# Two pairs of prompt blocks through the experts as a dense product over both tables, the other blocks by gathers

## The reference

```python
def peer_ffn(h, w_query, sub_keys, u_table, v_table):      # 1024 prompt tokens + 32 samples
    q = (hf @ w_query).reshape(-1, 8, 2, 128)
    s = einsum('nhpk,hpmk->nhpm', q, sub_keys)             # 8 heads, 2 halves, 128 keys
    sv, si = top_k(s, 16)
    comb = sv[:, :, 0, :, None] + sv[:, :, 1, None, :]     # 16 x 16 sums per head
    cidx = si[:, :, 0, :, None] * 128 + si[:, :, 1, None, :]
    fv, fpos = top_k(comb, 16)
    eid, gate = take(cidx, fpos), softmax(fv)
    # for each block of 128 tokens
    a = einsum('phkd,pd->phk', u_table[eid], h)            # u_table, v_table: 16384 x 1024
    act = gelu(a) * gate
    return einsum('phk,phkd->pd', act, v_table[eid])
```

## Time and profile before

| | |
|---|---|
| median of 3 runs | 3471.02 us (3469.92 to 3482.42) |
| span of the profiled execution | 3289.1 us |
| median less span | 181.9 us |
| busy: PE, DVE, POOL, ACT | 2159.5, 2139.4, 2280.5, 368.6 us |
| moved by DMA | 1235.08 MB, of which gathers 1109.40 MB |
| mean granted TensorE clock | 0.823 |

### The profile page before, as it was taken

One profiled execution on the slowest core, in us unless ns is written; L12 is line 12 of the kernel. 1 busy time (PEld: TensorE's weight loads), 2 busy tenths in 40 slices (PEclk: granted clock), 3 DMA queues, 4 the chain that ended last, 5 costly groups with the idle time before them and its releaser, 6 DMA issues.

```text
span 3289.1 us, 30699 instructions
## 1 busy us (share of the span) xinstructions
PE 2159.5 (66%) x9831; PEld 958.8 (29%) x9831; DVE 2139.4 (65%) x4892; ACT 368.6 (11%) x793; POOL 2280.5 (69%) x2229
## 2 busy tenths in 40 slices
PE   6885896756776468997855577767454445545556
PEld 5573442212443113453211143434111111111111
DVE  1577756676788855666575657877766666677431
ACT  2112231100010110222100100001000000000000
POOL 0144677776777777777776777777777777777765
PEclk9997998977887789999877688889767777667679
DMA  8778899999999999999999999999999999999998
GB/s 290 202 273 299 326 385 386 388 401 401 397 395 389 360 396 406 405 405 386 382 400 394 375 399 390 392 382 370 369 405 406 402 402 406 406 385 402 382 363 321
DMA packets 363454, 1235.08 MB, mean 376 GB/s; under 512 B 36855, under 2 KB 40335, under 8 KB 363279
## 3 DMA queue, kind: packets, MB, share of 16 engines
q0 software_dynamic: 304784, 1109.40, 87.4%
q1 hardware_dynamic: 36335, 79.69, 6.8%
q10 hardware_dynamic: 22176, 44.04, 3.6%
HBM read 1220.31 MB, written 13.28 MB: 375 GB/s over the span
## 4 chain that ended last, share of the span: by engine, by line
POOL 29%; DMA 27%; PE 24%; issue 11%; DVE 7%; DVEq 1%; ACT 1%; SPq 0%; POOLq 0%; ACTq 0%
DMA v_ring<-in_v_table_dram,eidt 21%; POOL u_ring L807 15%; POOL v_ring L827 14%; PE bank L1758 13%; DMA u_ring<-in_u_table_dram,eid 4%; PE bank L1586 3%; PE bank L1668 2%; DVE u_ring L1381 2%; PE bank L1569 2%; PE bank L1644 2%; DMA u_ring<-in_v_table_dram,eidt 1%; DVE mixt L1211 1%; DVE work L1272 0%; DMA u_ring<-in_w_ada_dram 0%; POOL u_ring L827 0%
## 5 line engine op out<-in xcount | busy, mean ns | idle before, releaser
L1758 PE MATMUL bank<-v_ring,act_x 128*32 128x512 f32 x4104 | 1177.7, 808 | 977.7 <-DMA v_ring<-in_v_table_dram,eidt 929.9
L1381 DVE CUSTOM_DVE_ANT_0 u_ring<-u_ring,h 128x1024 f32<-128x1024 f32 x1056 | 1279.5, 1226 | 785.4 <-DMA u_ring<-in_u_table_dram,eid 711.9
L807 POOL DMA_INDIRECT u_ring<-in_u_table_dram,eid x1024 | 1129.9, 1103 | 444.0 <-issue 312.2
L827 POOL DMA_INDIRECT v_ring<-in_v_table_dram,eidt x1026 | 1070.3, 1043 | 397.3 <-issue 245.8
L1758 PEld LDWEIGHTS bank<-v_ring,act_x 128*32 128x32 f32 x4104 | 271.4, 135 | 1794.3 <-issue 1785.0
L1668 PEld LDWEIGHTS bank<-hbuf,wring 128*128 128x128 f32 x1984 | 228.4, 194 | 22.0 <-issue 22.0
L1668 PE MATMUL bank<-hbuf,wring 128*128 128x128 f32 (+1 forms) x1984 | 234.4, 279 | 0.0
L1586 PE MATMUL bank<-zc,dring 128*128 128x384 f32 x496 | 193.3, 514 | 4.0 <-ACT dring L860 4.0
L1569 PE MATMUL bank<-hbuf,wring 128*128 128x384 f32 (+2 forms) x448 | 150.8, 495 | 22.7 <-DMA wring<-in_w_in_dram 13.7
L1644 PE MATMUL bank<-wring,mixt 128*128 128x512 f32 (+1 forms) x256 | 123.2, 631 | 0.0
L1569 PEld LDWEIGHTS bank<-hbuf,wring 128*128 128x128 f32 x448 | 85.7, 194 | 89.7 <-issue 50.8
(11 more groups left out here) (267 smaller groups left out, 1696.6 us busy)
## 6 DMA issues: line engine op xcount, KB each, us to landing
v_ring<-in_v_table_dram,eidt POOLq DMA_INDIRECT x1026, 6.9
u_ring<-in_u_table_dram,eid POOLq DMA_INDIRECT x1024, 6.8
wring<-in_w_out_dram ACTq DMA_DIRECT2D x16, 1024.0 KB, 11.9
wring<-in_w_query_dram ACTq DMA_DIRECT2D x16, 1024.0 KB, 11.7
wring<-in_w_in_dram ACTq DMA_DIRECT2D x10, 1024.0 KB, 11.8
xr<-in_x_prompt_dram SPq DMA_DIRECT2D x16, 512.0 KB, 7.4
v_ring<-in_w_ada_dram SPq DMA_DIRECT2D x7, 1024.0 KB, 13.4
wring<-in_w_ada_dram SPq DMA_DIRECT2D x5, 1024.0 KB, 5.6
```

Source lines behind the costliest of these rows:

```text
L807: pool.indirect_dma_start(u_ring[:, n % NU], None, u_table[0], bass.IndirectOffsetOnAxis(ap=col, axis=0)).then_inc(u_in[n % NU], 16)
L827: pool.indirect_dma_start(place, None, v_table[0], bass.IndirectOffsetOnAxis(ap=eidt[:, b % RING, t:t + 1], axis=0)).then_inc(landed, 16)
L1381: dve.tensor_tensor_reduce(u_ring[:, n % NU], u_ring[:, n % NU], h2[:, b % 2], 1.0, 0.0, ALU.mult, ALU.add, dot[:, b % 2, k:k + 1]).then_i ...
L1758: last = pe.matmul(acc[h][j * S:(j + 1) * S, :], act_x[:, i % 2, j, a:a + S], v_place(n)[0][:, h * HALF:(h + 1) * HALF], start=(c == 0), s ...
```

## The change

Blocks 2 and 3 are one **dense pair**, blocks 6 and 7 another. They are no longer gathered. Blocks 0, 1, 4, 5 and SB keep the path above (`POS`), so the loop has 160 slots. For a dense pair (256 tokens) there are two stages, put into slots by `lay_out_dense` behind the last step of mixer and queries:

- **Units** (64, ten to a slot). A unit makes the gates of 4 tokens as a 128x128 table of first and second key each. VectorE makes gate-weighted one-hot columns of the first key (4 instructions), ScalarE those of the second as relu(1 - |key - number|) (4 of 128x128 and one of 128x512), TensorE multiplies them (4 matmuls 128x128), ScalarE copies the bank into a stage of 16 tokens. Each full stage (1 MB) is stored to DRAM by SP in runs of 512 B; there are two stage buffers.
- **Rounds** (134, seven to a slot). A round loads 128 rows of u and of v (0.5 MB each), transposes the u tile in two halves (one bank, 7, each half copied out by ScalarE), multiplies it with the 256 tokens (8 matmuls of 256 columns into bank 6), applies gelu, multiplies on VectorE by the gates read back (1 MB per 8 rounds), and adds the product with the v tile into banks 2 to 5 (4 matmuls of 512 columns). The v product runs 6 rounds behind the load, the dots 3.

The token matmuls of a slot are split around half of its dense work. Mixer and queries are packed closer: `ROOM` is 12 and 13, most gaps are shorter, both halves of the key search stand in the slot of the scores. The v ring has 5 rows, the sixth keeps the dense pair's keys and gates. VectorE now runs the steps of the same slot as TensorE, where it was one slot behind (`DVE_LAG`). The end of each dense block (`finish`) stands in the same order of ends as those of the gathered blocks.

```diff
-NV = 6
+NV = 5
-ROOM = [None, 7, 4.6]
+ROOM = [None, 12, 13]
+POS = [0, 1, 4, 5, SB]
+DENSE = [[2, 3], [6, 7]]
+UNIT = 4
+STOK = 16
+GEN_UNITS, ROUNDS = (10, 10), (7, 7)
...
+def lay_out_dense(steps):
+    at = max(s for s, todo in enumerate(steps) if any(x[0] not in pieces for x in todo)) + 2
+    for r, bs in enumerate(DENSE):
+        at = max(at, max(s for s, todo in enumerate(steps) if ("nrm", PARTS - 1, bs[-1]) in todo) + 2)
+        slots[at] += [("numbers", r, q) for q in range(NDB)]
+        for u in range(NUNIT):
+            slots[at + u // GEN_UNITS[r]].append(("unit", r, u))
...
+        for m in range(NROUND):
+            slots[at + m // ROUNDS[r]].append(("round", r, m))
...
+            def unit(r, u):
+                pe.wait_ge(oh_i_ready, n + 1)
+                pe.wait_ge(oh_j_ready, n + 1)
+                if n >= 4:
+                    pe.wait_ge(unit_taken, n - 3)
+                for i in range(UNIT):
+                    last = pe.matmul(ps[2 + n % 4][:, i * P:(i + 1) * P], oh_j[:, n % 2, i], oh_i[:, n % 2, i], start=True, stop=True)
+            def tile_turned(n, h):
+                if n + h:
+                    pe.wait_ge(ut_ready, 2 * n + h)
+                for a in range(4):
+                    last = pe.transpose(ps[7][:, a * P:(a + 1) * P], ud[n % NUD][:, (4 * h + a) * P:(4 * h + a + 1) * P], ident[:, :])
+            def dense_round(r, m, s):
+                for h in range(2):
+                    if m < NTILE:
+                        tile_turned(r * NTILE + m, h)
+                    if 0 <= m - VD_LAG < NKEY:
+                        dense_values(r, m - VD_LAG, h)
+                if 0 <= m - NDB - 1 < NKEY:
+                    dense_dots(r, m - NDB - 1, s)
...
+            def second_keys(r, u):
+                for i in range(UNIT):
+                    act.activation(oh_j[:, n % 2, i], iota_e, ACT.Abs, bias=gij[:, q, 2, t + i:t + i + 1])
+                if u:
+                    unit_out(r, u - 1)
+                act.drain()
+                act.activation(oh_j[:, n % 2], oh_j[:, n % 2], ACT.Relu, bias=one_c, scale=-1.0).then_inc(oh_j_ready, 1)
...
+            def dense_weights(r, m):
+                    dve.wait_ge(ge_ready, n + 1)
+                    dve.tensor_tensor(w, w, gch[c % 2].rearrange("p b t i c -> p (b t) i c")[:, :, i % IC], ALU.mult).then_inc(wd_ready, 1)
```

More of the change, by code:

```diff
@@ L161, in lay_out @@
 def lay_out():
-    slots = [[] for _ in range((NB + 1) * NCH)]
+    slots = [[] for _ in range(NSLOT)]
     load = [0] * len(slots)
@@ L204, in spread @@
             last = int(at)
-            if i[0] == "turn" and (last - V_LAG) % LAG > LAG - 5:
+            if i[0] == "turn" and (last - V_LAG) % LAG > LAG - 6:
                 last = at = last + LAG - (last - V_LAG) % LAG
@@ L418, in build @@
+        ud_in = [sem(f"ud_in{i}") for i in range(NUD)]
+        vd_in = [sem(f"vd_in{i}") for i in range(NVD)]
+        ut_ps, ut_ready, a_ps, ge_ready, wd_ready, vd_ps, dacc_free = (
+            sem(n) for n in ("ut_ps", "ut_ready", "a_ps", "ge_ready", "wd_ready", "vd_ps", "dacc_free"))
         steps = lay_out()
-        DVE_LAG = 1
+        dense, dense_ends = lay_out_dense(steps)
+        ends, END_ORDER = lay_out_ends(dense_ends)
+        END_NO = {x: i for i, x in enumerate(END_ORDER)}
+        END_BLOCK = [POS[x[1]] if x[0] == "row" else DENSE[x[1]][x[2]] for x in END_ORDER]
@@ L421, in build, with dots_before, turns_before @@
         SPREAD_AT = (0, 1)
-        turned = [sum(1 for s_ in range(V_LAG + LAG * i) for step in steps[s_] if step[0] == "turn") for i in range(2 * NB)]
-        turned.append(2 * NB + 1)
+        def dots_before(s):
+            return sum(1 for todo in dense[:s] for x in todo if x[0] == "round" and 0 <= x[2] - NDB - 1 < NKEY)
+        def turns_before(s):
+            return sum(1 for todo in steps[:s] for x in todo if x[0] == "turn")
+        turned = [sum(1 for s_ in range(V_LAG + LAG * i) for step in steps[s_] if step[0] == "turn") for i in range(2 * NPP)]
@@ L1454, in _ @@
             norm(1)
-            for p in range(NB + 1):
+            for p in range(NPP + 1):
                 for c in range(NCH):
-                    if p < NB or c < NSG:
-                        chunk(p, c)
-                    slot = p * NCH + c - DVE_LAG
-                    for step in steps[slot] if slot >= 0 else []:
+                    todo = dense[p * NCH + c]
+                    for end in ends[p * NCH + c]:
+                        finish(end)
+                    for j in range(CH):
+                        if p < NPP or c < NSG:
+                            dots(p, c, j, j + 1)
+                        for step in todo[j * len(todo) // CH:(j + 1) * len(todo) // CH]:
+                            dense_step(*step)
+                    dve.drain()
+                    for step in steps[p * NCH + c]:
                         kind = step[0]
@@ new lines, in dense_dots @@
+            def dense_dots(r, i, s):
+                n = r * NKEY + i
+                pe.wait_ge(act_taken, halves(s))
+                pe.wait_ge(eidt_ready, turns_before(s))
+                pe.wait_ge(ut_ready, 2 * (r * NTILE + NDB + i + 1))
+                if n:
+                    pe.wait_ge(ge_ready, n)
+                for k in range(KC):
+                    last = pe.matmul(ps[6][:, DT:2 * DT], ut[i % 2][:, k * P:(k + 1) * P], ht[:, k, :], start=(k == 0), stop=(k == KC - 1))
+                last.then_inc(a_ps, 1)
@@ L1815, in _ @@
             modulation(11)
-            for p in range(NB + 1):
+            for p in range(NPP + 1):
                 for c in range(NCH):
+                    todo = dense[p * NCH + c]
+                    if p == NPP and c == NSG + 2:
+                        weights(NPP, 0, p * NCH + c)
                     if v_chunk(p * NCH + c):
```

519 lines of the change are left out of this document (409 added, 110 removed).

## The result

The changed kernel takes 4607.16 us, median of 4 runs (4603.28 to 4609.07), where before took 3470.47 (3461.77 to 3482.42): a ratio of 1.3269 [1.3224, 1.3313]. The prediction was 4512 us, 4300 to 4800. The profiled execution took 4608.27 us with a span of 4606.1.

The account below looks back on a forecast made before the run. It took the gather stream to bound the kernel before and TensorE the rounds after. 195.5 head + 1420 slots + 205 units + 1148 rounds + 205 units + 1105 rounds + 52 end = 4330 us, plus 182 gives 4512; range 4300 to 4800.

Parts of the forecast that it names:

- Rounds, 8.0 us each: Dense rounds: TensorE needs 3.50 us of dots, 3.56 of value matmuls and 0.95 of transposes, 8.0 us a full round.
- starts and ends: Round stages: 35 and 25 us for starts and waits, plus 10 and 4 us as the ends' share.
- handshake rival: Rounds: with one bank each for transposes and dots, 1.6 us a round of ScalarE stand bare; 4920 us, chance 0.09.
- clock rival: Rounds: each half tile's wait drops TensorE to 1.2 GHz half the time, 1000 us more; 5500 us, chance 0.03.
- The other side: Rounds: 128-column matmuls go two at a time, a round takes 4.5 us; 3610 us, at best 3420; chance 0.03.
- Slots 0 to 97, 1420 us: Slots before the dense stages: each slot goes at its longest engine, adding to 1509 us; taken as 1420, 1230 to 1560.
- the rings: Slots 0 to 97: rings of 5 and 6 rows let an engine run about a slot ahead, smoothing some of 1509 us.
- rival of better smoothing: Slots 0 to 97 go at VectorE's own sum, 1230 us; the kernel takes 4320 us, chance 0.15.
- Units, 205 us a stage: Unit stages: ScalarE longest at 2.7 us a unit; 12.8 us taken per 1 MB gate buffer filled, 205 us a stage.
- rival of slow stores: Units: stores in 512 B runs take 22 us per 1 MB stage buffer and bind; 4810 us, chance 0.08.
- Around the span, 182 us: Outside the span: 3471.0 less 3289.1 us, 181.9 us, kept as a fixed cost and added to the forecast span.
- turning point: Rounds: the round time, about 4.2 us, from which the prediction said it decides whether the change could be faster than before.

Follow-up runs that it names:

- e2: Changed kernel with the dots of a round over 4 of the 8 pieces of the contraction: 4140.01 us against 4587.
- e12: Changed kernel with the dots of a round as bfloat16 matmuls on bfloat16 copies of u tiles and tokens: 3930.64 us against 4587.
- e3: Changed kernel loading only 64 of 1024 columns of the table tiles beyond the first of each buffer: 4590.24 us against 4587.
- e6: Changed kernel with VectorE running the steps of the slot before, as before the change: 4490.63 us against 4587.
- e7: Changed kernel with POOL issuing a slot's v gathers ahead of its u gathers: 4510.93 us against 4587.
- e9: Changed kernel with three edits, later copy in the units, VectorE a slot behind and v gathered first: 4460.25 us against 4587.
- e5: The changed kernel, unchanged, run again beside the kernel before on the chip of the later runs: 4586.91 us, ratio 1.3897.
- e4: Changed kernel with ScalarE copying out the bank of the unit before the last, not of the last: 4482.46 us against 4587.
- e8: Changed kernel with the copy of a unit's bank written straight, so gates are stored in another order: 4525.61 us against 4587.
- e1: The kernel before, unchanged, with span and time from one execution: 3299.38 us with a span of 3297.4.

## Why the prediction was right, and where it was not

**The bound.** Right: the change takes 200 MB off a stream which was the bound and puts some 2000 us of float32 matmuls (256 x 6.88 + 260 x 0.88) on TensorE, which has no slack for them. e2 and e12 price the rounds by TensorE's instructions to 1% (437 us less in the rounds where 1024 x 0.431 is 442, and 654 where 256 x 2.58 is 660), and e3 takes half of the rounds' stream away at no gain. Two pairs of rounds took 2169 us; forecast 2253 with their gaps.

**Rounds, 8.0 us each.** Measured 7.76. From start to start the transposes take 0.88 us, the values 3.43 and the dots 3.45, where the rows had given 0.95, 3.56 and 3.50. At these prices the rounds and the token matmuls are 1071 and 1044 us, which leaves 32 and 22 us for starts and ends where 45 and 29 stood: priced too high as well. The handshake rival (4920) fell: TensorE is busy 997.7 of 1000 us and hardly waits for a copy, some 8 us in all rounds. The clock rival (5500) fell: 1.00 over 1000 us of rounds. The Trainium skill ("TensorE: Matmul & The Clock Gate", A second HAM failure mode) describes a clock that goes up and down in a kernel that cycles through banks with short idle times. The rounds cycle through banks but have hardly any idle time, 21 and 13 us in 1103 and 1066, so they do not test it; the units, where TensorE idles some 2 us between groups of matmuls into banks in turn, had a mean clock of 0.61, which fits it, though no run separates the banks from the idle time. The other side, dots two at a time, fell with e2: each of the 1024 dots taken out gave 0.427 us, where one takes 0.431 in a round.

**Slots 0 to 97, 1420 us.** This is the step that failed: 1646, above even its own upper end of 1560. I added each slot's longest engine, 1509, and took something off for the rings. Where VectorE leads alone its own work fills the slot (slots 36, 37, 39 and 40 took it 19.0, 15.0, 20.4 and 17.7 us, 16.8, 13.3, 17.4 and 15.3 of it busy and under 1 us in each waiting for another engine). But the change also made VectorE's steps those of the same slot as TensorE's, and where they need TensorE's result of that slot the shares come close to adding up instead of covering each other (slot 38, with scores: 24.6 us, 9.5 of it a wait for them; slot 85: 25.2 us for 15.8 and 12.4). I had named the removed lag in the change and given it no price. e6 puts it at 92 us, e7 puts POOL's order of issues at 70; e9 shows that these are not two separate sums. With the lag back (and the later copy) the part is 1521 us, close to the plain addition of 1509. So my 89 us off for the rings was not there in sum; whether they smooth nothing, or smooth some and another loss of like size stands against it, no run separates. Of 1646 us, 25 go with the first runs (the part is 1621 in e5), likely by slower gathers. That leaves 1621 - 1521 = 100 us to the lag, give or take the 10 us by which this part differs from run to run; what of those e7's order would win by itself, without the lag, overlaps with it and stays open. The rival of better smoothing (1230 us) fell.

**Units, 205 us a stage.** 270 measured. I added ScalarE's work at 2.7 us a unit and held the store to be the bound. It was neither: a unit was a chain of relu, matmuls and copy, 4.1 us, with the matmuls at a clock of 0.61 (2.05 us, priced at 0.9) and the copy at 1.04, priced at 0.60. e4 shows the chain (104 us for both stages), e8 the copy (61 us). I had expected ScalarE over 80% busy and TensorE under half; they were at 70% and 59%. The rival of slow stores (22 us a stage) fell: they were no bound at 16.9 us.

**Around the span, 182 us.** There is no such thing: 2.2 us. I took the difference of two executions of different speed for a fixed cost. The three errors in the span are +226, +129 and -84, and with this one of -180 they cancel to +95 us. The nearness of 4512 to 4607 is thus in part luck; the span was forecast at 4330 and is 4606, 6% more.

**Where the expected gain went.** The stream lost 200 MB, 530 us at before's 375 GB/s. But it was freed in stages that TensorE bounds, where nothing waits for it. Rounds and units take 2708 us, and since they can start only when the buffers of mixer and queries are free, all of mixer and queries is pressed into slots 0 to 97, which take 1646 us. By the average of 10.7 us I had 1050 us for 98 slots of before; its trace has slot 98 begin on VectorE at 1328.4 us, so they took 1133, and the close packing cost some 510 us, not 370. Head, slots 0 to 97, units and end are 195.5 + 1646 + 539 + 56 = 2437 us; to match the 3297 of e1, the 268 rounds would have (3297 - 2437) / 268 = 3.2 us each, about what the stream alone takes for one by the prediction's estimate (3.0), and less than the 4.2 us that the prediction gave as the turning point.

## What to carry to other kernels

A gather costs bandwidth; its dense replacement costs matmuls over the whole table, and in float32 that was 7.8 us of TensorE for 1.05 MB of tables, which with their gates are an estimated 3 us of the stream. Before such an exchange, divide the matmul time of a tile by its transfer time. When steps of several engines share a slot, a sum of longest engines supposes that each works on what another finished a slot earlier; take that lag away, and in slots where one needs the other's result the time goes towards the sum of their shares. Here that was about 100 of 1621 us. And a time around the span is read from one execution, never from the median of one set of runs and the span of another.

## What the runs showed of the hardware

- The kernel bound by gathers took 3470 us in the first runs and 3289 to 3303 on three chips later, 5% apart; the one bound mostly by TensorE 4607 and 4587, 0.4% apart. Why is not shown.
- A ScalarE copy of 128x512 float32 out of a bank took 0.60 us with straight writes (e8) and 1.04 with writes 64 B apart.
- Float32 matmuls of 256 columns took 0.43 to 0.44 us each, bfloat16 ones 0.13 (8 in 1.04), both with 128-column weights at a granted clock of 1.00.
- TensorE with 2.05 us of matmuls every 4 us had a mean granted clock of 0.61, so mostly the lower level of 1.2 GHz; in the rounds, without such waits, it was 1.00.
